# Four of eight steps in the seven-product form instead of three, and the products combined at the panel's end

## What is computed

```python
# first block, twice
h = rms_norm(x, norm_g)
u = h @ w_in                          # ends in 4 gates of 2048 columns each
for n, (y, z) in enumerate(branches): # attention, retention, recurrence, memory
    branch = y * silu(z)
    merged = merged + sigmoid(gate_all[:, :, n]) * (branch @ w_branch[n])
x = x + merged @ w_out
# second block, once: attentions, gates, w_o, and then
gt, up = split(rms_norm_2(x, g_ffn) @ w_gate_up, 2)
x = x + (silu(gt) * up) @ w_down
```

## Time and profile before

| | |
|---|---|
| median of 3 runs | 3276.46 us (3275.17 to 3276.5) |
| profiled execution | 3276.25 us |
| its span, first to last instruction | 3274.5 us |
| granted TensorE clock over the span | 1.00 |
| PE busy | 3261.5 us, 15091 matmuls |
| DVE busy | 2201.4 us (67%) |
| ACT busy | 1638.1 us (50%) |
| chain that ended last | PE 100% |

### The profile page before, as it was taken

The page is one execution under the profiler, slowest core; times in us unless marked ns, Lnnn a source line. Parts: engine busy times, 40 slices in busy tenths (PEclk is TensorE's granted clock), DMA queues, the critical chain, the costliest instruction groups (busy, mean ns, idle before and its releaser), DMA issues.

```text
span 3274.5 us, 39927 instructions
## 1 busy us (share of the span) xinstructions
PE 3261.5 (100%) x15091; PEld 2702.4 (83%) x15091; DVE 2201.4 (67%) x2476; ACT 1638.1 (50%) x2085; POOL 321.2 (10%) x282
## 2 busy tenths in 40 slices
PE   8999999999999999999999999999999999999999
PEld 7888888888888888888888888888888888888887
DVE  5466655588865656555888655575555578888886
ACT  6444445455544444454555545455444455555554
POOL 0111241100000102411000011160000100000000
PEclk9999999999999999999999999999999999999999
DMA  8665565666656655556666675554565666566554
GB/s 300 190 184 167 165 176 162 188 207 195 217 190 206 180 168 167 174 164 189 200 206 189 209 221 172 172 178 146 193 190 183 186 214 202 182 193 211 188 186 161
DMA packets 303807, 619.77 MB, mean 189 GB/s; under 512 B 24960, under 2 KB 29440, under 8 KB 302464
## 3 DMA queue, kind: packets, MB, share of 16 engines
q1 hardware_dynamic: 303616, 617.22, 61.1%
HBM read 609.80 MB, written 7.34 MB: 188 GB/s over the span
## 4 chain that ended last, share of the span: by engine, by line
PE 100%; DMA 0%; DVE 0%; ACT 0%; SPq 0%; issue 0%
PE G L1127 69%; PE X L1046 7%; PE X L1048 7%; PE X L1047 6%; PE X L826 2%; PE G L1048 2%; PE G L1047 2%; PE G L1046 2%; PE X L942 1%; PE X L914 1%; PE G L1121 1%; PE X L969 0%; PE X L968 0%; PE X L935 0%; PE X L916 0%; PE X L889 0%
## 5 line engine op out<-in xcount | busy, mean ns | idle before, releaser
L1456 DVE TENSOR_TENSOR w_lo<-raw,w_hi 128x1024 fp32r<-128x1024 f32 (+1 forms) x902 | 1105.7, 1228 | 918.2 <-ACT w_hi L1152 893.7
L1152 ACT ACTIVATE w_hi<-raw 128x1024 fp32r<-128x1024 f32 (+1 forms) x902 | 936.6, 1042 | 1204.3 <-PE G L1127 1048.8
L1127 PE MATMUL G<-w_hi,xh 128*128 128x512 f32 x1984 | 797.0, 402 | 0.0
L1127 PE MATMUL G<-w_hi,xl 128*128 128x512 f32 x1984 | 776.0, 391 | 0.0
L1127 PE MATMUL G<-w_lo,xh 128*128 128x512 f32 x1984 | 773.8, 390 | 0.0
L1127 PE MATMUL G<-w_hi,yh 128*128 128x512 f32 x1104 | 440.2, 399 | 8.4 <-DVE w_lo L1456 8.4
L1127 PEld LDWEIGHTS G<-w_hi,xl 128*128 128x128 f32 x1984 | 372.6, 188 | 80.6
L1127 PEld LDWEIGHTS G<-w_hi,xh 128*128 128x128 f32 x1984 | 373.3, 188 | 73.5 <-issue 2.6
L1127 PEld LDWEIGHTS G<-w_lo,xh 128*128 128x128 f32 x1984 | 373.8, 188 | 71.9
L1127 PE MATMUL G<-w_hi,yl 128*128 128x512 f32 x1104 | 432.8, 392 | 0.0
L1127 PE MATMUL G<-w_lo,yh 128*128 128x512 f32 x1104 | 431.4, 391 | 0.0
(11 more groups left out here) (261 smaller groups left out, 3644.8 us busy)
## 6 DMA issues: line engine op xcount, KB each, us to landing
raw<-in_w_in SPq DMA_DIRECT2D x572, 512.0 KB, 3.6
raw<-in_w_gate_up SPq DMA_DIRECT2D x122, 512.0 KB, 4.0
raw<-in_w_down SPq DMA_DIRECT2D x66, 512.0 KB, 5.2
raw<-in_w_out SPq DMA_DIRECT2D x64, 512.0 KB, 4.2
raw_more<-in_w_gate_up SPq DMA_DIRECT2D x54, 512.0 KB, 4.7
raw_more<-in_w_in SPq DMA_DIRECT2D x52, 512.0 KB, 4.4
raw<-in_w_branch SPq DMA_DIRECT2D x48, 512.0 KB, 3.8
raw<-in_w_mem_kv SPq DMA_DIRECT2D x32, 512.0 KB, 6.2
```

The source lines that it names most:

```text
L1127: mm = M.matmul(G[blk.g][:, t, :], a[:, blk.kk + k, tok], ringed(w, blk, c)[:, j, :], start=(k == 0 and q == 0), stop=(k == blk.kt - 1 and ...
L1152: A(high_of(c)[:, 0:size_of(c)], source_of(c), ACT.Copy).then_inc(hi_done, 1)
L1456: V.tensor_tensor(low_of(c)[:, 0:n], source_of(c), high_of(c)[:, 0:n].bitcast(F32), ALU.subtract).then_inc(lo_done, 1)
```

## The change

`SEVEN` becomes (0, 2, 4, 6). Matmuls that were never the first on their bank now are (banks `PT[0]`, `PT[1]`, `PS` in step 0), and the plain steps' start flags follow; bank `PO` is first written in plain step 1. In DVE's loop `cross` is put ahead of `read_out`, because both now fall behind the same unit: the last "sums24" is two units ahead of the panel's last. `x_forms` and the stage "forms" go over the four entries.

```diff
-SEVEN = (1, 3, 5)
+SEVEN = (0, 2, 4, 6)
...
                     if what == "low":
-                        three(PT[0], *by_token(2 * s + 1, 0), c, 0, False, False)
-                        mm = three(PT[1], *by_form(l, s, 3), c, 1, False, False)
+                        three(PT[0], *by_token(2 * s + 1, 0), c, 0, s == 0, False)
+                        mm = three(PT[1], *by_form(l, s, 3), c, 1, s == 0, False)
...
-                        mm = three(PS, *by_token(2 * s + 1, 1), c, 1, False, False)
+                        mm = three(PS, *by_token(2 * s + 1, 1), c, 1, s == 0, False)
...
-                                mm = three(bank, *by_token(s, t), c, h, c == blk.first, end)
+                                mm = three(bank, *by_token(s, t), c, h, s == (2 if bank is PO else 0), end)
...
                 for e in BEHIND[c]:
+                    if e - 2 in STEM_ENDS:
+                        cross(STEM_ENDS[e - 2])
                     if e in ENDS:
                         read_out(ENDS[e])
-                    if e - 2 in STEM_ENDS:
-                        cross(STEM_ENDS[e - 2])
```

## The result

| | before | changed |
|---|---|---|
| median | 3276.13 us | 3363.4 us |
| profiled execution | 3276.25 us | 3364.4 us |
| its span | 3274.5 us | 3362.6 us |
| granted clock, mean | 1.000 | 0.994 |
| PE busy, matmuls | 3261.5 us, 15091 | 3278.9 us, 15034 |

A forecast was written before the change was run, and what follows sets the result against it. PE, busy 100% of the span, was taken as the bound; -12.9 us for saved matmuls and +80.6 for waits at panel borders made +67.7 on 3276.25, forecast 3344 us, range 3320 to 3368.

The forecast's parts named there:

- the -12.9: PE over 19 panels: 57 matmuls fewer, each worth its distance to the next, saves 12.9 us.
- The added work of DVE: Each panel: +4.2 us of DVE, 49.2 of 51.7 us in a layer, still fits and costs nothing by its sum.
- The fourth set of forms: Feed-forward group's start: may hold the panel under 1 us, covered by the later wait for G1, so costs nothing.
- The borders: Where panels meet: early seven-product start and cross directly ahead of gather make PE wait, +80.6 us in all.
- Layers: Eight periods between a layer's panels: waits of 0.5 for G0 and 3.3 for G1, less 0.68; +3.1 each, +24.6 us.
- Feed-forward: Eight periods: two down read-out waits of 1.6 and 1.3, G1 1.3, less 0.68; +3.5 each, +28.2 us.
- First panels: First panel of each of three groups: G1's read-out stands behind three splits, 3.5 us each, +10.6 us.
- two m_feed waits: Last panel of each layer: PE's first m_feed wants the gather at 5.5, gets it at 7.8; +4.6 us for two.
- the price of the clock: PE behind the new waits: the forecast's sum added nothing for matmuls running at the lower clock.
- C: Rival, 8%: each of 11 waits over 3 us brings twelve matmuls at 1.2 GHz, 2.4 us; +26, 3372 us.
- Rival A: Panel borders hide and PE stays the bound, so only the saved matmuls count: 3263 us; chance 4%.
- Rival B: Only G1's early-start waits are paid, 1.3 us at 16 borders, 3.5 at three; cross and gather hide: 3295 us; 9%.

The follow-up runs named there:

- experiment 3: Changed kernel with the four seven-product steps at 1, 3, 4 and 5, so neither end of a panel is touched; 3268.94 us, ratio 0.9979 to the kernel before.
- experiment 1: Changed kernel with only three seven-product steps, at 0, 2 and 4: early panel start, cross where it stood before; 3312.09 us, ratio 1.0110 to the kernel before.
- experiment 2: Changed kernel with three seven-product steps, at 1, 3 and 6: plain panel start, cross directly ahead of gather; 3297.67 us, ratio 1.0066 to the kernel before.
- experiment 8: experiment 3 with the feed-forward part's sets of activation forms every 5 units instead of 6; 3267.32 us, ratio 0.9975 to the kernel before.
- experiment 4: Changed kernel with the three matmuls ahead of each layer panel's first G1 wait issued four times more; 3348.85 us, ratio 1.0223 to the kernel before.
- experiment 7: experiment 3 with feed-forward forms every 5 units instead of 6 and m_feed stages one chunk later; 3270.11 us, ratio 0.9982 to the kernel before.
- experiment 5: experiment 4 with two repeats of the three matmuls instead of four; 3350.97 us, ratio 1.0229 to the kernel before.
- experiment 6: Changed kernel with DVE reading out an ended merge or down block ahead of the split, not behind it; 3304.53 us, ratio 1.0086 to the kernel before.

## Why the prediction was right, and where it was off

**What bounds, and the -12.9: right.** 15034 matmuls; experiment 3 shows the gain where no border is touched.

**The added work of DVE costs nothing by its sum: right.** Experiments 1 and 2 are slower with no work added, experiment 3 is faster with all of it.

**The fourth set of forms: nearly.** It held the first feed-forward panel by 0.8 us, hidden behind the wait for G1 as said; with the border waits gone it is 1.2 us of its own (experiment 3), and a spacing of 5 takes that away (experiment 8).

**The borders: right in place, order and size.** Layers: 3.1 for G1 and 0.5 for G0 (3.3 and 0.5 forecast). Feed-forward: the two down waits 1.4 and 1.5 idle, G1 0.8 idle (1.6, 1.3, 1.3 forecast); by distances the period's growth is 3.8 against 3.5. First panels 3.3 (3.5), at the third 2.2 for G1 behind the 1.0 for the forms; two m_feed waits 2.2 and 2.6 by distances (2.3 each). The walk to m_feed is as forecast in the changed kernel, but the forecast put the wait down to the late cross alone, and experiments 2 and 3 show that the two added units, which move that gather behind two more splits, are needed for it and make waits without the late cross. Together 78.5 by distances, 80.6 forecast. Two numbers in it were loose and went against each other. PE went on 713.46 - 713.40 = 0.06 us after DVE's result, where 0.28 was taken from the start of the kernel; the 0.1 of the next matmul comes on top. And the layer's stretch in the earlier trace rows, called a period, was 0.5 us short of one: from gather to gather it is 52.86. The growth was worked out from the waits, not from that figure, so nothing else hangs on it.

**The step that failed: the price of the clock.** The sum had it at nothing, and C, which had it at 26, got 8%, because "No row shows a later fall [...], nor a later wait to cause one". That was no evidence against it: a trace without waits can't show what waits do to the clock, and the only row that bore on it, the start of the kernel, spoke for C. The term measured some 18 us in the profile and 18.3 between the two profiled executions of experiment 4. The prediction's own sign for C, matmuls 0.43 us apart behind the waits, is there after eight of ten waits for G1, and 3363.4 lies nearer to C's time than to the forecast's. C's price for one fall, 2.4 us from twelve slow matmuls, was too high, and its count of 11 near enough: ten stretches, nine of 1.7 us and one of 3.0. (Its time of 3372 is 2 us over its own sum, 3344 + 26.) With the measured 18 the forecast's sum would have been 3276.25 + 67.7 + 18 = 3362, against the profiled execution's 3364.4. That the time lies in the range is partly luck: the range's upper side was made for read-outs placed otherwise, 18 us, and what filled it was the clock. The Trainium skill's rule (TensorE: Matmul & The Clock Gate, HAM oscillation), that waits between groups of matmuls can put the clock back each time, agrees with the rows at 711 and 1592 us (granted clock 0.72 and 0.62); the rows at 653 and 1650 us (1.00), behind waits as long, show that it need not happen each time.

**Rival A** falls by every wait for G1, and with it what was drawn from the most-contended engine alone: PE at 100% before says what a matmul is worth as long as the order around it holds. **Rival B** priced the floor, an early start alone, at 31 us without the saved matmuls; experiment 1, which has just that, measured 36, the clock's 3.4 among them. With the late cross beside it the waits are more than twice as long.

What stays open: what decides whether a given wait is followed by the lower clock. Waits of 3.1 us were and weren't (eight of ten in the changed kernel, two of three in experiment 1), those of 2.2 to 2.6 at m_feed were in two profiles and weren't in three others, one of 2.0 in experiment 7 was, those of 1.7 to 2.2 for G1 in experiments 5 and 6 never were.

## What to carry to other kernels

In a kernel whose engines keep a written order, an engine at 70% can still set the time: look at what is queued between the event that frees a bank and the instruction that reads it out, and at how much work the waiting engine has left until it needs the bank. An edit that makes the last use and the first use of a bank meet at a border should be walked through with start times before it is tried; the same saving inside the loop (steps 1, 3, 4, 5) was worth 7 us, and 8 with the forms spaced closer, where this one cost 87. Look at the last panel of a group by itself: two more units in a panel moved its gather behind two more splits. When waits of microseconds are newly made in front of matmuls, add to the sum what TensorE may lose at its lower clock behind them, here 1.7 us for most.

## What the runs showed of the hardware

Nine of ten stretches at 1.2 GHz in the changed kernel cost 1.7 us each, whether the wait ahead was 3.1 us or 2.2; one, at 1594 us, was twice as long and cost about 3.0. Filling the waits with matmuls that nobody needs made the kernel 14.6 us faster. With the layers' waits filled, the same kernel's executions lay in two groups, two at 3346 us with a granted clock of 1.000 over the span and two at 3352 us with 0.998 and 0.999. So the number of such stretches seems to vary between executions of one kernel; only the profile of a 3346 us one is there to look at.
